# Eight accumulator slots, a staggered denominator chain and bulk loads on SyncE in an encoder block

## The reference

```python
xn = rms_norm(h, norm_mix_g[l])
proj = xn @ w_in[l]                                   # [B, S, IN_WIDTH]
u, vg, q, k, va, gate_a, gate_b = jnp.split(proj, splits, axis=-1)
y_gmlp = spatial_gating(u, vg, gmlp_ln_g[l], gmlp_ln_b[l], gmlp_ws[l], gmlp_bs[l])
y_attn = dilated_attention_mixer(q, k, va).astype(h.dtype)
merged = (jax.nn.sigmoid(gate_a) * (y_gmlp @ w_branch_gmlp[l])
          + jax.nn.sigmoid(gate_b) * (y_attn @ w_branch_attn[l]))
h = h + merged @ w_out[l]
h = h + swiglu(rms_norm(h, norm_ffn_g[l]), w_ffn_gate[l], w_ffn_up[l], w_ffn_down[l])
```

## Time and profile before

| | us |
|---|---|
| median of 3 runs | 2565.79 (2563.62 to 2570.7) |
| the profiled execution | 2563.62 |
| its span on the slowest core, core 4 | 2562.5 |
| spans of the other cores | 2546.1 to 2562.0 |
| PE busy on core 4 | 2424.5 (95%) |
| DVE, ACT, POOL busy | 1060.0, 769.2, 520.1 |

### The profile page before, as it was taken

How to read it: one execution, slowest core, us unless ns; L and a number is a source line. 1 busy time by engine, 2 the same in 40 slices (tenths; PEclk the granted TensorE clock), 3 DMA queues, 4 the chain that set the end, 5 groups by cost and what they waited for, 6 DMA issues and landing times.

```text
span 2562.5 us, 38646 instructions; the slowest of 8 cores (2546.1 to 2562.5 us)
## 1 busy us (share of the span) xinstructions
PE 2424.5 (95%) x12989; PEld 1216.3 (47%) x13248; DVE 1060.0 (41%) x1717; ACT 769.2 (30%) x1159; POOL 520.1 (20%) x639
## 2 busy tenths in 40 slices
PE   5987899999989889999999999999999999999998
PEld 2444455556546434444444444444444444444443
DVE  2545656777657644323333433323222222323222
ACT  2534545554434412122122212222121212222111
POOL 2111200345454433132222223000000000000000
PEclk9998999999999989999999999999999999999999
DMA  8999975465676545246325428812111120201001
GB/s 175 224 226 223 227 184 140 102 111 102 115 163 146 156 157 124 67 67 130 97 36 124 111 47 197 277 60 75 42 58 66 42 74 25 83 28 72 34 34 41
DMA packets 178163, 285.75 MB, mean 112 GB/s; under 512 B 51105, under 2 KB 127521, under 8 KB 176930
## 3 DMA queue, kind: packets, MB, share of 16 engines
q1 hardware_dynamic: 133842, 203.27, 28.5%
q0 software_dynamic: 32704, 64.27, 15.5%
q10 hardware_dynamic: 11424, 15.73, 2.1%
HBM read 250.14 MB, written 104.54 MB: 138 GB/s over the span
## 4 chain that ended last, share of the span: by engine, by line
PE 72%; DMA 16%; POOL 4%; issue 3%; DVE 2%; SPq 2%; ACT 1%; POOLq 0%; ACTq 0%; DVEq 0%
PE ps L210 68%; DMA sb<-rdens 5%; DMA sb<-x 5%; DMA rdens<-sb 2%; POOL sb L763 2%; POOL sb L737 2%; SPq L117 1%; PE ps L509 1%; PE ps L490 1%; DMA sb<-sb 1%; PE ps L245 1%; DMA sb<-acc 1%; DMA sb<-xnt 1%; DMA k2s<-sb 1%; PE ps L1085 1%
## 5 line engine op out<-in xcount | busy, mean ns | idle before, releaser
L210 PE MATMUL ps<-sb 128*128 128x512 bf16 x9829 | 2232.6, 381 | 59.6 <-DVE sb L448 15.3
L210 PEld LDWEIGHTS ps<-sb 128*128 128x128 bf16 x10088 | 984.1, 99 | 1163.0 <-issue 77.9
L497 DVE SCALAR_TENSOR_TENSOR ps<-sb,ps 128x512 f32<-128x512 f32 x384 | 266.5, 694 | 112.4 <-PE ps L490 90.4
L1304 DVE TENSOR_TENSOR sb<-ps,sb 128x512 bf16<-128x512 f32 x176 | 121.6, 691 | 410.0 <-PE ps L210 348.7
L500 ACT ACTIVATE sb<-ps 128x1024 bf16<-128x1024 f32 x192 | 196.6, 1024 | 307.6 <-DVE ps L497 207.8
L233 POOL TENSOR_TENSOR sb<-sb 128x1 f32<-128x1 f32 x104 | 58.4, 561 | 1131.8 <-DVE sb L231 1131.8
L229 ACT ACTIVATE sb<-sb 128x1024 bf16<-128x1024 f32 x104 | 109.6, 1053 | 378.8 <-DVE sb L1319 291.8
L1303 ACT ACTIVATE sb<-ps 128x512 bf16<-128x512 f32 x176 | 105.0, 596 | 390.1 <-PE ps L210 387.1
L509 PE MATMUL ps<-sb 128*128 128x128 bf16 x1536 | 123.3, 221 | 25.8 <-DVE sb L709 15.8
L1101 ACT ACTIVATE sb<-ps 128x512 bf16<-128x512 f32 x128 | 76.1, 596 | 222.1 <-PE ps L210 219.7
L1111 DVE SCALAR_TENSOR_TENSOR sb<-sb,ps 128x512 f32<-128x512 bf16 x64 | 44.0, 687 | 237.3 <-PE ps L210 237.3
(11 more groups left out here) (65 smaller groups left out, 1079.0 us busy)
## 6 DMA issues: line engine op xcount, KB each, us to landing
sb<-x SPq DMA_DIRECT2D x72, 512.0 KB, 10.0
sb<-hres SPq DMA_DIRECT2D x64, 512.0 KB, 3.5
wfb<-wff POOLq DMA_DIRECT2D x33, 512.0 KB, 19.2
sb<-wfb SPq DMA_DIRECT2D x33, 512.0 KB, 13.8
hres<-sb SPq DMA_DIRECT2D x32, 512.0 KB, 3.1
y<-sb SPq DMA_DIRECT2D x32, 512.0 KB, 2.6
wmb<-wmx POOLq DMA_DIRECT2D x104, 128.0 KB, 4.6
sb<-xnt POOLq DMA_DIRECT2D x32, 384.0 KB, 6.9
```

The lines of the kernel that those rows point to most:

```text
L210: tk.op("pe", lambda e: e.matmul(out, lhsT, rhs, start=start, stop=stop), R=R, W=PK(b), sig=sig)
L497: tk.op("dve", lambda e: e.scalar_tensor_tensor(out=p4, in0=m4, scalar=u["slope"][s], in1=p4, op0=ALU.mult, op1=ALU.add), R=kk + MTAB.keys ...
L1304: tk.op("dve", lambda e: e.tensor_tensor(out=AT[fc].ap, in0=PS(bks[1]), in1=sg.ap, op=ALU.mult), R=PK(bks[1]) + sg.keys, W=AT[fc].keys)
```

## The change

It has five parts. (1) The prologue: the loads of the first four blocks of x are issued at once and not behind pieces of weights; the norms, transposes and projections of the first blocks are recorded in another order (block 1's square sum before block 0's scaling; each block's projection behind its transposes); the first weights after W2[1] are issued after block 1's square sum, not block 2's; a memset of VST2 stands behind the two copies of GMIX; a k or q projection waits for the whole tile of weights, not for its quarter. (2) Eight accumulator slots in place of four; for w > 0 the loads stand one w ahead. (3) The chain's steps f1, f3, f4, f5 stand 1, 6, 10, 17 half-steps behind the last addition in place of 1, 4, 7, 11, the store has a step of its own (f6), and the broadcast load is one DMA in place of two. (4) Slabs and all bulk loads are issued from SP. (5) The weights of the gates, of u and of v have other places in memory, and so other times: gate a's weights are loaded at w = 8, not at w = 6.

```diff
-    ACT_ = [[bf(o + 2 * s, 2, F32) for s in range(2)] for o in (178.25, 182.25, 198.25, 186.25)]
+    ACT_ = [[bf(o + 2 * s, 2, F32) for s in range(2)]
+            for o in (154.25, 158.25, 162.25, 166.25, 178.25, 182.25, 198.25, 186.25)]
...
-    WV = [bf(10.25, 8), bf(18.25, 8)]
-    WU = [bf(34.25, 8), bf(42.25, 8)]
-    WGB = [bf(26.25, 8), bf(50.25, 8)]
-    WGA = [bf(154.25, 8), bf(162.25, 8)]
+    WV = [bf(34.25, 8), bf(42.25, 8)]
+    WU = [bf(154.25, 8), bf(162.25, 8)]
+    WGB = [bf(10.25, 8), bf(18.25, 8)]
+    WGA = [bf(26.25, 8), bf(50.25, 8)]
...
-    bq = dict(q="pool")
+    bq = dict(q="sp")
...
-    load_x(1, XB[0].keys)
-    load_x(2, W2[1].keys[0:8])
-    load_x(3, W2[1].keys[8:16])
+    for blk in range(1, 4):
+        load_x(blk)
...
-                    mm(PS(b), w3[:, kc, c * 128:(c + 1) * 128], x3[:, kc, :], wv.keys[4 * kc:4 * kc + 4] + xn.keys, b,
+                    mm(PS(b), w3[:, kc, c * 128:(c + 1) * 128], x3[:, kc, :], wv.keys + xn.keys, b,
...
-            i = (w * 4 + c) % 4
+            i = (w * 4 + c) % 8
...
-                    if gu == 1:
-                        if c < 3:
-                            load_acc(c + 1)
-                        elif w < 7:
-                            nxt[w + 1](0)
+                    if w == 0 and gu == 1 and c < 3:
+                        load_acc(c + 1)
+                    if gu == 2 and w < 7:
+                        if c > 0:
+                            nxt[w + 1](c - 1)
+                        if c == 3:
+                            defer(6, lambda: nxt[w + 1](3))
...
-            for s in range(2):
-                tk.dma("sp", rb.ap[64 * s:64 * s + 64, :], rd_d[j, s:s + 1, :].partition_broadcast(64), R=[("dr", "rd", j)],
-                       W=rb.keys, stream="rdi%d" % (c % 2), joined=(s == 1))
+            tk.dma("sp", rb.ap, rd_d[j].unsqueeze(1).broadcast_to([2, 64, 512]), R=[("dr", "rd", j)],
+                   W=rb.keys, stream="rdi%d" % (c % 2))
...
             defer(1, f1)
-            defer(4, f3)
-            defer(7, f4)
-            defer(11, f5)
+            defer(6, f3)
+            defer(10, f4)
+            defer(17, f5)
+            if c == 3:
+                defer(18, f6)
...
-                tk.dma("pool", s3[:, 2 * i:2 * i + 2, :], xnt_d[:, 2 * i:2 * i + 2, lo:lo + 768], R=R,
+                tk.dma("sp", s3[:, 2 * i:2 * i + 2, :], xnt_d[:, 2 * i:2 * i + 2, lo:lo + 768], R=R,
...
     norm0(0)
-    norm1(0, False)
-    norm2(0)
     norm0(1)
-    norm1(1, False)
-    norm2(1)
-    norm0(2)
-    norm1(2, False)
+    norm1(0)
     wload(W2[0], CH_K + 2, "w2_0", now=True)
-    load_x(4, W2[0].keys[0:8])
-    load_x(5, W2[0].keys[16:24])
-    load_x(6)
...
+    for blk in range(4):
+        if blk < 3:
+            norm1(blk + 1)
+        norm2(blk)
+        norm0(blk + 2)
+        if blk == 1:
+            wload(W2[2], CH_Q + 2, "w2_2", now=True)
+        first_v[blk]()
```

More of the change, by code:

```diff
@@ L304, in build_program @@
     T2B = [bf(202.25 + 2 * i, 2, F32) for i in range(2)]
-    slots = ([10.25 + 4 * i for i in range(4)] + [34.25 + 4 * i for i in range(4)] + [154.25 + 4 * i for i in range(4)]
+    slots = ([34.25 + 4 * i for i in range(4)] + [154.25 + 4 * i for i in range(4)] + [10.25 + 4 * i for i in range(4)]
              + [26.25, 30.25, 50.25, 54.25] + [70.25 + 4 * i for i in range(4)] + [178.25, 182.25, 66.25]
@@ L372, in build_program @@
     wload(W2[1], CH_VA + 2, "w2_1", now=True)
-    load_x(1, XB[0].keys)
-    load_x(2, W2[1].keys[0:8])
-    load_x(3, W2[1].keys[8:16])
-    for i in range(4):
-        tk.op("dve", lambda e: e.memset(VST2[i].ap, 1.0), W=VST2[i].keys)
+    for blk in range(1, 4):
+        load_x(blk)
     tk.op("pool", lambda e: e.memset(MHALF.ap, -0.5), W=MHALF.keys)
@@ L385, in build_program @@
         tk.op("dve", lambda e: e.tensor_copy(out=GMIX.ap[:, hf * 512:(hf + 1) * 512], in_=PS(b)), R=PK(b), W=GMIX.keys)
+    for i in range(4):
+        tk.op("dve", lambda e: e.memset(VST2[i].ap, 1.0), W=VST2[i].keys)
     rs_of = {}
@@ L390, in norm0, with norm1 @@
         rs_of[blk] = rstd_of(XB[blk % 4], XS[blk % 4])
-    def norm1(blk, ld=True):
+    def norm1(blk):
         scale_rows(XB[blk % 4], rs_of.pop(blk), GMIX, XS[blk % 4], "dve")
-        if ld and blk + 4 < NTOK // 128:
+        if blk + 4 < NTOK // 128:
             load_x(blk + 4)
@@ L651, in load_acc @@
                 R = [("dr", "a2", h, w // 4, rg) for rg in range(4)]
-                if w == 0:
+                if w < 2:
                     tk.op("pool", lambda e: e.memset(a.ap, 0.0), W=a.keys)
@@ L659, in g01_units @@
         for c in range(4):
-            i4 = (w * 4 + c) % 4
+            i4 = (w * 4 + c) % 8
             for gu in range(4):
@@ L764, in f5, with f6 @@
                           R=a.keys + rb.keys, W=yb.keys, rows=(64 * s, 64))
-            if c == 3:
-                tk.dma("sp", yt_d[w], yb.ap.rearrange("p (c t) -> p c t", c=4), R=yb.keys, W=[("dr", "yt", w)],
-                       stream="yto%d" % (w % 2))
+        def f6():
+            tk.dma("sp", yt_d[w], yb.ap.rearrange("p (c t) -> p c t", c=4), R=yb.keys, W=[("dr", "yt", w)],
+                   stream="yto%d" % (w % 2))
         late = w == 7 and c == 3
@@ L825, in build_program @@
     norm0(0)
-    norm1(0, False)
-    norm2(0)
     norm0(1)
-    norm1(1, False)
-    norm2(1)
-    norm0(2)
-    norm1(2, False)
+    norm1(0)
     wload(W2[0], CH_K + 2, "w2_0", now=True)
-    load_x(4, W2[0].keys[0:8])
-    load_x(5, W2[0].keys[16:24])
-    load_x(6)
-    first_v[0]()
-    norm2(2)
-    norm0(3)
-    norm1(3)
-    wload(W2[2], CH_Q + 2, "w2_2", now=True)
-    first_v[1]()
-    norm2(3)
-    norm0(4)
-    first_v[2]()
-    norm0(5)
-    first_v[3]()
+    for blk in range(4):
[6 more added lines that the diff above has]
+        first_v[blk]()
     norm1(4)
@@ L997, in build_program @@
                     for hf in range(2):
-                        wget(WGB[hf], CH_GB + hf, "wgb%d" % hf)
+                        wget(WGA[hf], CH_GA + hf, "wga%d" % hf)
                 if i == 1:
@@ L1004, in build_program @@
                 if i in (5, 9):
-                    wget(WV[i // 9], CH_V + i // 9, "wv%d" % (i // 9))
-                if i == 12:
-                    wget(WU[0], CH_U, "wu0")
+                    wget(WGB[i // 9], CH_GB + i // 9, "wgb%d" % (i // 9))
             g()
@@ L1017, in build_program @@
             if w == 6 and i == 0:
-                for hf in range(2):
-                    wget(WGA[hf], CH_GA + hf, "wga%d" % hf)
                 bulk.append(lambda: load_xn(0))
@@ L1185, in build_program @@
         if oc == 0:
-            wget(WU[1], CH_U + 1, "wu1")
+            for hf in range(2):
+                wget(WV[hf], CH_V + hf, "wv%d" % hf)
+        if oc == 6:
+            for hf in range(2):
+                wget(WU[hf], CH_U + hf, "wu%d" % hf)
         if oc == 4:
```

7 lines of the change are left out of this document (4 added, 3 removed).

## The result

The changed kernel takes 2530.5 us (median; 2565.8 before), 0.9857 of the time before, interval 0.9833 to 0.988. In a later set of runs it took 2521.2 against 2551.7: 0.9887, 0.985 to 0.9924. So it is faster by 1.1 to 1.4%. The forecast was 2541 us, in a range from 2522 to 2565. Executions in which one die showed a far lower clock are left out of every number here.

The account below looks back on a forecast made before the run. PE was taken to be held by accumulator loads late behind SP's waits for POOL's inversion. Core 4 gains 13 + 11 + 7.5 + 3 = 34.5, to 2528; core 0 gains 15, to 2537.9, giving 2541 us, range 2522 to 2565.

Parts of the forecast that it names:

- Accumulator waits go, PE fills from 650 to 900 us: DVE's 31.4 us wait for acc goes near zero; core 4 gains 13 and 11 us, core 0 none and 4.
- The sign that I had set for being wrong: Wrong if accumulator loads come in time and PE still idles 10 us or more in 650 to 900.
- What takes them away: Accumulator loads standing 27 to 29 half-steps ahead of their first addition, in place of 13, remove the waits for acc.
- SP's wait for the inversion far below 179.4: SP's 179.4 us of waiting for POOL's inversion falls far, its place taken by waits for the accumulator's addition.
- The tail, 7.5 us: Last stretch, waits for POOL's products: 5 us of PE waits and 2.5 of clock, 7.5 on core 4, 8 on core 0.
- rival 3: SP stays one blocked line, so gate weights come late and some 17 us come back: 2558 us; chance 0.08.
- Rival 1: The one load back, on two DMA engines, lands in 11 to 13 us; the tail's gain goes: 2551 us; chance 0.13.
- Rival 2: The two engines of the load back become the bound, from 6.5 us a load: 2586 us; chance 0.09.
- Rival 4: The prologue gives its full 6.6 us and the tail 3 us more: 2534 us; chance 0.10.
- Prologue, 3 us: Loads issued early fill the transfer gap between 16 and 28 us: gain of 3, ends 6.6 gained and 5 lost.
- Core 0 becomes the slowest: Core 0 gains only 15 us, to 2537.9, core 4 34.5, to 2528, so core 0 sets the time.
- Bulk loads on SP cost nothing: About two more issues a round on SP are hidden by its idle waits; costed at nothing.

Follow-up runs that it names:

- e4: Changed kernel with accumulator loads issued at the old place, two units ahead of their first addition; 2527.4 us against 2565.1 before, ratio 0.9893.
- e11: Changed kernel with the chain's old distances and the reciprocals loaded back as two loads; 2526.0 us against 2551.7 before, ratio 0.9892.
- e6: Changed kernel with the reciprocals loaded back as two loads in place of one; 2515.5 us against 2558.8 before, ratio 0.983.
- e12: Kernel before with only the load back of reciprocals made one load; 2661.1 us against 2551.7 before, ratio 1.0434.
- e1: Kernel before with the new prologue alone; 2558.9 us against 2565.1 before, ratio 0.9976.
- e8: Changed kernel with slabs, gate weights and the last stage's first loads issued by POOL, not SP; 2536.5 us against 2558.8 before, ratio 0.9913.
- e2: Changed kernel with the old prologue; 2541.9 us against 2565.1 before, ratio 0.9939.

## Why the prediction came out as it did

- *Accumulator waits go, PE fills from 650 to 900 us:* right, but smaller. The 31.4 us of DVE's wait are 0 on every core. From the 3600th weight load to the 5200th (631 to 879 us) core 4 took 247.8 us before and 230.6 after, 17.2 less, where 24 were priced (13 and 11). The mean over the cores fell by 13, from 243.5 to 230.1: core 4 had the longest wait for acc of all, and my sum took its bad luck for the kernel's cost. The sign that I had set for being wrong, accumulator loads in time and PE still idle for 10 us or more from 650 to 900, did come: 15.9 us on core 4 (1.3, 6.6 and 8.0 in the three stretches; 26.3 before). Only 2.8 us of it are waits for additions. The changed kernel is some 29 us ahead at 850, so that the tail's wait for L753 (4.1 us, at 877) now falls before 900, and the wait for the gate weights (3.0 us, at 817) is new. The sign should have been tied to a stretch of work, not of time.
- *What takes them away:* a wrong step in part. I gave it to the lead of 27 to 29 half-steps. e4 has the old lead and no wait, so the rest of the change does it without the lead. With the old distances the waits are gone in e11, which has the lead and two loads; how much of that is the lead stays open. The prediction looked at SP's blocked queue, but didn't add up the circle that blocks it.
- *"SP's wait for the inversion far below 179.4":* right, 83.2, with waits for L711 in its place.
- *The tail, 7.5 us:* from the 5200th to the 5600th weight load core 4 took 94.6 us and then 89.3, 5.3 less. L760's wait went, L752's (now L753) grew from 3.6 to 10.0 on that core. The gate weights cost PE another 2 to 3 us before that stretch, a small form of rival 3.
- *Rival 1, which I gave 0.13, was true in its mechanism.* It expected a landing of 11 to 13 us; 10.6 from issue to product was measured (the profile has no landing for this load), and L753's wait grew by 6.4 us (6 expected). e6 prices it at 11 to 15 us of mean span, above the 10 that lie between its 2551 and my 2541. The Trainium skill, "DMA: Bandwidth & Descriptors", section "Rules for kernel authors", says that an outermost dimension smaller than 16 keeps a transfer on at most that many engines. The trace agrees with it: of the 128 packets of 2 KB of one load 1.7 at a time were under way on the mean and never more than 4 (twelve loads of the changed kernel), of those of two loads 7.0 and up to 20 (e6), and they took 7.5 us from the first to the last, against 3.1. The prediction had 7.5 us by bytes. The trace doesn't name the engines, so that it is two isn't shown. That the time still came out below the forecast is due to the prologue and the spread, below.
- *Rival 2, the bound from 6.5 us a load:* it did not come, although the load takes longer than that; the acc loads land in 4.4 us (median; 6.0 before). But one part of the change, its one load, does cost over 100 us without the new distances (e12), by another mechanism: a circle of waits, not full engines.
- *Rival 4, 2534:* half right. The prologue gave its 6.6 us and more, but the tail gave less than forecast, not more. That its number lies nearest to the 2530.5 measured is in part luck.
- *Prologue, 3 us:* mis-sized; 7.6 measured in e1, and 9 to 13 ahead at the 1200th weight load. I priced only the idle transfers (6.6 at best) and left out what PE loses from 25 to 75 us: 12.2 us idle on core 4 and 5.3 by the clock of 0.86 (0.14 x 37.8).
- *Core 0 becomes the slowest:* the step that failed most. From one execution I took 15 us for core 0 and 34.5 for core 4, and core 0 gained 35.1 (2552.9 to 2517.8, one execution each). It had been held back by its clock of 0.81 from 75 to 175 us, which the prediction didn't read. The cores are alike on the mean, so the time falls by the fall of the mean span (19.3) and of the spread (10.6): 29.9 of the 30.5 us measured in the second pair. The sum for core 4 met its 2528 only as a mean gain and a lucky draw together.
- *Bulk loads on SP cost nothing:* they gain 6 to 8 us (e8), since at the end it is POOL that is waited for.

## What to carry to other kernels

Before a term is read from the slowest of eight like cores, look at the same wait on the others: what differs from core to core is spread, and a change that removes it gains twice, in the mean and in the slowest. A chain that goes through two in-order queues is to be drawn as a circle with its sum beside the round it must fit in; a transfer that grows by 4 us cost over 100 us here while the circle had one round, and 11 to 15 once it had two. Splitting one broadcast load in two again was the best edit of all, so every part of a change that gains deserves a run without it.

## What the runs showed of the hardware

- One load of two rows of 64 copies (256 KB) was awaited 10.6 us from its issue (median, core 7 of the changed kernel), two loads of one row each 5.7 (core 4 of e6). Its 128 packets were under way 1.7 at a time, those of the two loads 7.0.
- In one execution two neighbouring cores stayed at a granted clock of 0.81 for 100 us with PE full (100.00 of 100); with the same prologue in e2 and e12 all eight were at 1.00 there. Their clock records hold 0.812 without a break from 69 to 215 us, neither of the two levels, 1.0 and 0.5, between which the other cores' records go.
- The span of the slowest core lies 1.0 to 1.1 us below the execution's time in every kernel.
